# First passes behind the fourth and fifth norm over tiles without the root, and gate sums as two scans

## The chip, the cores and the metric

The kernel runs on one core of one Trainium2 chip. Its time is device time in microseconds. TensorE (PE) multiplies matrices and writes PSUM, VectorE (DVE) and ScalarE (ACT) do the elementwise work, GpSimd (POOL) adds a few squares, and SyncE (SP) issues the loads of the weights. Each engine works through its own list in a fixed order, and semaphores join the lists.

## The reference

Two blocks run one after the other on 256 tokens of width 1024, all in float32. The part that matters begins at the end of the first block: its last feed-forward (`ffn2`), its final norm, then the first (even) layer of the second block and the start of its second (odd) layer.

```python
x = x + 0.5 * ml[8] * swiglu(modulate(rms_norm(x, norm3_g), ml[6], ml[7]), ffn2_w_in, ffn2_w_out)
x = rms_norm(x, final_g)
...
def even_layer(x, ...):                       # second block, layer 0
    h = rmsnorm(x, pre_g)                     # the fourth norm
    u = h @ w_in
    qa, ka, va, oa, za, ia, fa, qb, kb, vb, zb = split_cols(u, EVEN_SPLITS)
    qk = silu(causal_dwconv(concatenate([qa, ka]), conv_w))
    ig = ia + b_i
    lf = log_sigmoid(fa + b_f)
    ha = mlstm(qa, ka, va, ig, lf)            # 4 heads: running sum of lf, running maximum
    ...
    return x + rmsnorm(y @ w_out, post_g)     # the post norm
def odd_layer(x, ...):                        # second block, layer 1
    h = rmsnorm(x, pre_g)                     # the fifth norm
    p, z = split(h @ w_in)                    # p is pooled over windows of 2, 4, 8, 16 tokens
    ...
```

A norm multiplies each token by one number, 1/root(mean of squares). A product with weights is linear, so that number may multiply the product instead of the input.

## The kernel before

**Products.** Channels lie on partitions and tokens along the free dimension. Each float32 operand is split into a high part (type fp32r) and the rest, and a product is three matmuls: high by high, low by high, high by low. A load brings 512 rows by 256 columns of a weight, a chunk, into one of six slots of `W`. The step `split` makes it usable: ACT copies it to `WH` (line 1298), DVE subtracts that to give `WL` (line 1645). `WH` and `WL` hold four chunks, so ACT's copy of a chunk waits until PE has finished the chunk four places back. With 8 rows of 128 inputs, a product of 256 columns takes two chunks of 24 matmuls each. PSUM banks 0 to 3 hold the product tiles in turn (`plan.tiles`), banks 4 to 6 the small work, bank 7 (`NB`) the sums of squares.

**The list.** The class `Plan` writes one list of steps, and every engine walks it and takes out its own part. `gemm` emits the chunks of one product, keeps the splits three to four chunks ahead (`LOOK`), and after each chunk calls `tick`, which takes one step of the generators in `self.back` (at most three in turn). `drain` runs them all to their end, with no chunk between.

**The fourth norm.** The last `fx2` tiles (feed-forward 2) are added into `X` by DVE (line 1528). ACT squares them twice (`square`, line 1129), PE sums the squares over the partitions with a matrix of ones (`ones`, line 842). The step `norm` follows: PE fills the time with seven matmuls that nobody reads (`warm`, line 899) and waits for the roots; ACT, DVE and ACT take the two roots (the final norm and the fourth norm follow each other, so there are two); DVE takes the reciprocal (line 1761), then writes eight times x by scale by reciprocal into `TS` (line 1492), ACT copies each to `XH` (line 1143), DVE subtracts to give `XL` (line 1500). Only then come the gates' 24 matmuls with 8 columns (`gr`, lines 1011 to 1013), and the products `eq`, `ek`, `ev`, `eo`, `ez` of head 0, 48 matmuls each, then those of heads 1 to 3.

**The gates.** The generator `gates` moves the gate rows through the steps g0, g1 (line 1017 on PE, then Abs, Exp, Ln on ACT at lines 1397 to 1401), three steps g2 (running sum by eight shifted additions, line 1632), three g3 (running maximum, likewise) and g4 (two small transposes, line 1022). Beside it runs `final_x` (nine steps that scale `X` by the final norm, line 1778). The generator `mlstm` of a head starts when g4 is done: m0 (lines 1029 to 1038), two ticks later m1 (1045 to 1053), five later m2 (1058). `drain` is called at the end of each head's products from head 1 on.

**The fifth norm.** Behind the output product `p0` the step `post` normalises the product: DVE multiplies by the reciprocal (line 1789) and adds to `X` (line 1795), ACT squares, PE sums; `norm` again makes the root and eight normalised tiles. Then come the products `op` (to be pooled, DVE lines 1588 to 1601, then `PH` and `PL`), `oz` (to `OZ`), 48 matmuls each, and after six of them the mixing product `om` from `PH` and `PL`.

## Time and profile before

| | us |
|---|---|
| median of 3 runs (lowest, highest) | 1418.59 (1418.24, 1421.0) |
| the profiled execution, its own time | 1421.97 |
| its span, first to last instruction | 1420.2 |
| PE busy | 1351.3 |
| DVE busy | 904.4 |
| ACT busy | 647.6 |

The profile is of one execution. Its time stands 3.4 us above the median; 1.8 us of it lie outside the span. A matmul row's duration overlaps that of its neighbours, so the distance of starts counts, not the duration. "PEclk" is the granted clock of TensorE as a share of 2.4 GHz: 1.00 is 2.4 GHz, 0.50 is 1.2 GHz. A row names what ended the idle time before it in brackets.

### The profile page before, as it was taken

What the parts mean: (1) busy time and instruction counts of PE and PEld (TensorE: products, weight loads), DVE (VectorE), ACT (ScalarE), POOL (GpSimd) and SP (SyncE); (2) the same over time, 40 slices, a digit from 0 to 9 for tenths busy, and PEclk for the clock granted to TensorE, in tenths of its full rate; (3) what the DMA queues carried; (4) which work ended last, traced back from release to release, by engine and by line L of the source; (5) the groups of instructions that cost most, each with busy time, mean ns of one, the idle gap of its engine ahead of it and who ended that gap; (6) DMA issues with size and microseconds to landing.
All of it is one profiled execution on the core that took longest, in us unless ns stands there. A gap on an engine that the chain in (4) does not pass through costs nothing.

```text
span 1420.2 us, 23299 instructions
## 1 busy us (share of the span) xinstructions
PE 1351.3 (95%) x9344; PEld 1224.1 (86%) x9344; DVE 904.4 (64%) x1448; ACT 647.6 (46%) x1017; POOL 25.2 (2%) x29
## 2 busy tenths in 40 slices
PE   6999999999997999999999999899899999999996
PEld 3688888888886799999989999788899999999996
DVE  3546456653476477766776655688776665487864
ACT  3522221222244335455554444565665765465553
POOL 0000000000100000000000000100000000000000
PEclk7999999999999999999999999999999999999998
DMA  7743434634344244366747765465345554536561
GB/s 260 263 147 119 149 133 148 193 104 155 119 157 133 75 142 153 124 206 225 266 162 240 240 190 177 119 178 163 106 146 150 149 155 127 164 119 192 181 196 42
DMA packets 201403, 229.67 MB, mean 162 GB/s; under 512 B 7120, under 2 KB 191696, under 8 KB 201296
## 3 DMA queue, kind: packets, MB, share of 16 engines
q1 hardware_dynamic: 201008, 227.90, 50.7%
q8 instruction: 74, 1.21, 0.4%
q10 hardware_dynamic: 288, 0.29, 0.1%
q14 instruction: 33, 0.27, 0.1%
HBM read 227.11 MB, written 1.05 MB: 161 GB/s over the span
## 4 chain that ended last, share of the span: by engine, by line
PE 54%; DVE 7%; ACT 3%; DMA 3%; issue 2%; SPq 0%; POOL 0%; ACTq 0%; DVEq 0%; POOLq 0%
PE P L880 15%; PE P L881 14%; PE P L882 14%; DMA W<-in_ffn_w_in 2%; ACT WH L1298 2%; PE P L886 1%; PE P L888 1%; PE P L887 1%; DVE WL L1645 1%; PE P L1001 1%; PE P L989 1%; PE P L842 1%; DVE TS L1492 1%; PE P L994 0%; PE P L972 0%
## 5 line engine op out<-in xcount | busy, mean ns | idle before, releaser
L1645 DVE TENSOR_TENSOR WL<-W,WH 128x1024 fp32r<-128x1024 f32 x358 | 432.1, 1220 | 302.7 <-ACT WH L1298 301.8
L880 PE MATMUL P<-XH,WH 128*128 128x256 f32 (+1 forms) x1808 | 560.1, 310 | 9.2 <-DVE XL L1502 4.2
L881 PE MATMUL P<-XL,WH 128*128 128x256 f32 (+1 forms) x1808 | 546.9, 303 | 0.0
L882 PE MATMUL P<-XH,WL 128*128 128x256 f32 (+1 forms) x1808 | 546.6, 302 | 0.0
L1298 ACT ACTIVATE WH<-W 128x1024 fp32r<-128x1024 f32 x358 | 368.9, 1043 | 249.1 <-PE P L882 128.4
L880 PEld LDWEIGHTS P<-XH,WH 128*128 128x128 f32 x1808 | 342.6, 189 | 36.8 <-issue 14.4
L881 PEld LDWEIGHTS P<-XL,WH 128*128 128x128 f32 x1808 | 341.6, 189 | 19.8 <-issue 2.9
L882 PEld LDWEIGHTS P<-XH,WL 128*128 128x128 f32 x1808 | 341.4, 189 | 17.1
L880 PE MATMUL P<-GH,WH 128*128 128x256 f32 (+1 forms) x372 | 123.0, 331 | 0.0
L882 PE MATMUL P<-GH,WL 128*128 128x256 f32 (+1 forms) x372 | 122.3, 329 | 0.0
L881 PE MATMUL P<-GL,WH 128*128 128x256 f32 (+1 forms) x372 | 122.3, 329 | 0.0
L880 PEld LDWEIGHTS P<-GH,WH 128*128 128x128 f32 x372 | 70.0, 188 | 7.4 <-DVE WL L1645 0.3
L881 PEld LDWEIGHTS P<-GL,WH 128*128 128x128 f32 x372 | 70.1, 188 | 7.1 <-issue 0.2
L882 PEld LDWEIGHTS P<-GH,WL 128*128 128x128 f32 x372 | 70.0, 188 | 6.9
L1168 ACT ACTIVATE GH<-TS 128x512 fp32r<-128x512 f32 (+1 forms) x44 | 22.7, 526 | 107.5 <-DVE TS L1518 107.5
L1709 DVE CUSTOM_DVE_ANT_0 W<-W,AC,V 128x1024 f32<-128x1024 f32 x56 | 71.6, 1279 | 0.0
L1518 DVE TENSOR_TENSOR TS<-TS,P 128x512 f32<-128x512 f32 (+1 forms) x44 | 23.9, 552 | 66.0 <-PE P L882 66.0
L1162 ACT ACTIVATE TS<-P 128x512 f32<-128x512 f32 (+1 forms) x44 | 21.0, 488 | 74.0 <-PE P L882 74.0
L1103 POOL TENSOR_TENSOR SQ<-SQ 128x256 f32<-128x256 f32 (+1 forms) x25 | 25.0, 1000 | 1373.2 <-ACT SQ L1129 1372.1
L886 PE MATMUL P<-WH,XH 128*128 128x256 f32 x160 | 46.3, 290 | 0.0
L887 PE MATMUL P<-WL,XH 128*128 128x256 f32 x160 | 45.6, 285 | 0.0
L888 PE MATMUL P<-WH,XL 128*128 128x256 f32 x160 | 45.5, 285 | 0.0
(290 smaller groups left out, 1816.6 us busy)
## 6 DMA issues: line engine op xcount, KB each, us to landing
W<-in_ffn_w_in SPq DMA_DIRECT2D x88, 512.0 KB, 5.5
W<-in_w_in_ab SPq DMA_DIRECT2D x72, 512.0 KB, 3.8
W<-in_w_modt SPq DMA_DIRECT2D x56, 512.0 KB, 4.0
W<-in_w_in SPq DMA_DIRECT2D x52, 512.0 KB, 4.5
W<-in_ffn_w_out SPq DMA_DIRECT2D x40, 512.0 KB, 4.8
W<-in_w_in_c SPq DMA_DIRECT2D x32, 512.0 KB, 4.0
W<-in_w_mod SPq DMA_DIRECT2D x16, 512.0 KB, 4.7
W<-in_w_out_ab SPq DMA_DIRECT2D x16, 512.0 KB, 3.6
```

What stands on the lines that cost most here:

```text
L880: pe.matmul(o, h[:, k, c], xh[:, kk, a:b], start=kk == 0, stop=False)
L881: pe.matmul(o, h[:, k, c], xl[:, kk, a:b], start=False, stop=False)
L882: mm = pe.matmul(o, l[:, k, c], xh[:, kk, a:b], start=False, stop=kk == gm.nk - 1)
L886: pe.matmul(o, xh[:, kk, c], h[:, k, :], start=kk == 0, stop=False)
L887: pe.matmul(o, xh[:, kk, c], l[:, k, :], start=False, stop=False)
L888: mm = pe.matmul(o, xl[:, kk, c], h[:, k, :], start=False, stop=kk == gm.nk - 1)
L1103: pool.tensor_tensor(SQ[:, 0, 0:n], SQ[:, 0, 0:n], SQ[:, 1 + (k - 1) % 2, 0:n], ALU.add) \
L1168: act.activation(GH[m][:, f % 12, :], TS[:, f % NS, 0:n], ACT.Copy).then_inc(S[f"hh{m}"], 1)
L1298: act.activation(h, a, ACT.Copy).then_inc(S["wh"], 1)
L1518: dve.tensor_tensor(TS[:, f % NS, 0:n], TS[:, f % NS, 0:n], ps, ALU.mult).then_inc(S[f"hm{m}"], 1)
L1645: dve.tensor_tensor(l, a, h.bitcast(F32), ALU.subtract).then_inc(S["wl"], 1)
L1709: td = dve.tensor_tensor_reduce(a if v == s.c - 1 else JK[:, :, :], a, (AC0, AC1)[v][:, :, :], 1.0, vec("bmod", 8 * g + k), ALU.mult, ALU. ...
```

## The change

- While `fx2` ends, ACT and DVE also make `XH` and `XL` (their columns 0 to 255, free at that time) from x by scale, without the root: the function `raw`. `eq` and `ek` of head 0 and the gates' rows run over these (type `raw` of the Gemm). So do `op` and `oz` of group 0 behind the fifth norm, where the step `pk` joins the additions of `post` with `raw`.
- Each of these eight tiles, and the gates' rows, is multiplied by the reciprocal when DVE takes it out of PSUM (`rooted`, line 1629 of the new file, and step g0), and ACT then works from SBUF.
- The normalised tiles are still made, four at a time (step `nm`), in between, for the products that follow. `warm` behind the fourth and the fifth norm is gone; behind the post norm ten of them stay in one piece.
- The gates' running sum and maximum are one scan instruction each; g2 and g3 are one step. The memory that is cleared for them shrinks. Of the two gate chunks only 8 columns are split.
- `final_x` starts after the fourth head's generator is added.

```diff
+    def even_start(self, eq, ek, ce, cg, ck):
+
+        self.half(eq, 0, ce[0], -1)
+        self.half(eq, 4, ce[1], 0)
+        self.step("o4")
+        self.half(eq, 4, ce[1], 1, 0)
+        self.step("r4")
+        self.nb_free = ("tw", 2)
+        self.split_chunk(ck[0])
+        b, f = self.bank(("gfree", 1))
+        for c, j in enumerate(cg):
+            self.marks += 1
+            self.chunk_end[j] = self.marks
+            self.step("gr", chunk=j, k0=4 * c, nk=4, bank=b, free=f)
+        self.ended("gr")
+        self.back.append(self.gates(b))
+        self.step("rx", gemm=eq)
+        self.split_chunk(ck[1])
+        self.tick()
+        self.step("nm", a=4, b=0)
+        self.half(ek, 0, ck[0], -1)
+        self.tick()
+        n = self.chunks[ck[1]][0]
+        self.split_to(n + 1)
+        self.step("nm", a=4, b=4)
+        self.half(ek, 4, ck[1], -1, 0)
+        self.tick()
+        self.split_to(n + 2)
+        self.step("ev", gemm=eq)
+        self.step("cvt", gemm=eq)
+        self.step("rx", gemm=ek)
+        self.tick()
+        self.split_to(n + 3)
+        self.step("cvr", gemm=eq)
+        self.step("ev", gemm=ek)
+        self.step("cvt", gemm=ek)
+        self.tick()
+        self.step("cvr", gemm=ek)
...
+        self.post(0)
+        self.step("pk", a=0)
+        self.half(op[0], 0, cp[0], -1)
+        self.step("pk", a=4)
+        self.half(op[1], 0, cp[1], -1)
+        self.split_chunk(cp[3])
+        self.split_chunk(cz[0])
+        self.step("o6", a=0)
+        self.half(op[0], 4, cp[2], -1, 0)
+        self.step("o6", a=4)
+        self.split_chunk(cz[1])
+        self.step("r5", b=self.root("n", 5))
+        self.half(op[1], 4, cp[3], -1, 0)
+        self.step("rx", gemm=op[0])
+        self.split_chunk(cz[2])
+        self.half(oz[0], 0, cz[0], -1)
+        self.step("ev", gemm=op[0])
+        self.step("rx", gemm=op[1])
+        self.step("nm", a=5, b=0)
+        self.split_chunk(cz[3])
+        self.half(oz[0], 4, cz[1], -1, 0)
+        self.step("opp", gemm=op[0])
+        self.step("rx", gemm=oz[0])
+        self.step("ev", gemm=oz[0])
+        self.step("nm", a=5, b=4)
+        self.half(oz[1], 0, cz[2], -1)
+        n = self.chunks[cz[3]][0]
+        self.split_to(n + 1)
+        self.step("ev", gemm=op[1])
+        self.half(oz[1], 4, cz[3], -1, 0)
+        self.step("opp", gemm=op[1])
+        self.split_to(n + 2)
+        self.step("rx", gemm=oz[1])
+        self.step("ev", gemm=oz[1])
+        self.split_to(n + 3)
...
-            self.gemm("ev", h, WAB, 0, 8, 2048 + 256 * h, LAT, turned=False)
+            if h:
+                self.gemm("eq", h, WAB, 0, 8, 256 * h, LAT)
+                self.gemm("ek", h, WAB, 0, 8, 1024 + 256 * h, LAT)
+            self.gemm("ev", h, WAB, 0, 8, 2048 + 256 * h, LAT, turned=False, first=h == 0)
             self.gemm("eo", h, WAB, 0, 8, 3072 + 256 * h, LAT)
             self.gemm("ez", h, WAB, 0, 8, 4096 + 256 * h, LAT)
             if h:
                 self.call(self.drain)
             self.call(lambda h=h: self.back.append(self.mlstm(h)))
+        self.call(lambda: self.back.append(self.final_x()))
...
-        for i in range(3):
-            self.step("g3", a=i)
-            yield
+        self.step("g2")
...
+            def raw(k, scale):
+
+                act.activation(XH[:, k, 0:T], X[:, k, 256:512], ACT.Copy, scale=scale).then_inc(S["xh"], 1)
...
+                                act.wait_ge(S["am"], 4)
+                                raw(k, AM[:, 2, 1, k:k + 1])
...
+            def raw(q, k, scale):
+
+                dve.wait_ge(S["xh"], q + 1)
+                dve.scalar_tensor_tensor(XL[:, k, 0:T], X[:, k, 256:512], scale, XH[:, k, 0:T].bitcast(F32), ALU.mult,
+                                         ALU.subtract).then_inc(S["xr"], 1)
...
+            def rooted(gm):
+
+                kind, i = gm.kind, gm.i
+                dve.wait_ge(S["dv"], inverse)
+                for j, t in enumerate(gm.tiles):
+                    k = 2 * i + j
+                    dve.wait_ge(S["g"], plan.tile_end[t])
+                    if kind[0] == "e":
+                        c = 2 * (kind == "ek") + j
+                        dve.wait_ge(S["gz"], 1)
+                        if c >= 3:
+                            dve.wait_ge(S["cvs"], c - 2)
+                        o = CV[:, c % 3, 3:T + 3]
+                    elif kind == "op":
+                        if k >= 2:
+                            dve.wait_ge(S["opc"], k - 1)
+                        o = PV[:, 3 * (k % 2), 16:16 + T]
+                    else:
+                        o = OZ[:, k, :]
+                    dve.tensor_tensor(o, P[:, t % 4, 0:T], RS[:, 0, 256:512], ALU.mult).then_inc(S["rx"], 1)
...
+                elif s.kind == "r4":
+                    r2 = RS[:, 0, 256:512]
+                    dve.wait_ge(S["on"], stat["s4"][2] + 3)
+                    dve.tensor_copy(r2, NB[:, T:2 * T]).then_inc(S["dv"], 1)
+                    own += 1
+                    dve.wait_ge(S["dv"], own)
+                    dve.scalar_tensor_tensor(r2, NB[:, 0:T], EPS, r2, ALU.mult, ALU.add).then_inc(S["two"], 1)
+                    dve.wait_ge(S["tw"], 1)
+                    dve.reciprocal(r2, r2).then_inc(S["dv"], 1)
+                    own += 1
+                    inverse = own
+                elif s.kind == "r5":
+                    r = RS[:, 0, 256:512]
+                    dve.wait_ge(S["sr"], s.b)
+                    dve.reciprocal(r, r).then_inc(S["dv"], 1)
+                    own += 1
+                    inverse = own
+                elif s.kind == "nm":
+                    dve.wait_ge(S["dv"], inverse)
+                    dve.wait_ge(S["am"], 4)
+                    dve.wait_ge(S["g"], end["hx", 2] if s.a == 4 else end["even"])
+                    tiles(s.a, s.b, s.b + 4, lambda k: vec("pre1", k) if s.a == 5 else AM[:, 2, 1, k:k + 1],
+                          lambda k: None, RS[:, 0, 256:512])
...
+                elif s.kind == "pk":
+                    for k in range(s.a, s.a + 4):
+                        add(0, k)
+                        if k > s.a:
+                            raw(7 + k, k - 1, vec("pre1", k - 1))
+                    raw(8 + k, k, vec("pre1", k))
...
+                    ig, b, t2, top, neg = (G[:, i, 128:384] for i in range(5))
+                    dve.wait_ge(S["gfree"], 1)
+                    dve.tensor_scalar(top, b, 0.0, None, ALU.min).then_inc(S["dv"], 1)
+                    own += 1
+                    dve.wait_ge(S["dv"], own)
+                    dve.wait_ge(S["gab"], 3)
+                    dve.tensor_tensor_scan(b, top, t2, 0.0, ALU.add, ALU.subtract).then_inc(S["dv"], 1)
+                    own += 1
+                    dve.wait_ge(S["dv"], own)
+                    dve.wait_ge(S["gr0"], 2)
+                    dve.tensor_tensor(t2, ig, b, ALU.subtract).then_inc(S["gq"], 1)
+                    dve.wait_ge(S["gq"], 1)
+                    dve.tensor_tensor_scan(top, t2, t2, 0.0, ALU.max, ALU.max).then_inc(S["dv"], 1)
+                    own += 1
+                    dve.wait_ge(S["dv"], own)
+                    dve.tensor_scalar(neg, top, -1.0, None, ALU.mult).then_inc(S["dv"], 1)
+                    own += 1
+                    dve.wait_ge(S["dv"], own)
+                    dve.tensor_tensor(G[:, 5, 128:384], neg, b, ALU.subtract).then_inc(S["gq"], 1)
```

**ACT, the gates of the even layer.** `WH` is a chunk's split, `Ev`, `Ek`, `TS`, `XH` are tiles as above, `G` the gates' rows. Before:

```order
L1298 ACTIVATE WH<-W 128x1024 [waits s_g,s_w5]
L1409 ACTIVATE Ek<-TS 128x256 [waits s_cvs] x2
L1397 ACTIVATE G<-G 4x256 [waits s_gfree]
L1399 ACTIVATE G<-G 4x256 [waits s_gab]
L1401 ACT_TABLE_LOAD
L1401 ACTIVATE G<-G 4x256 [waits s_gab]
L1298 ACTIVATE WH<-W 128x1024 [waits s_g,s_w0]
L1230 ACTIVATE Ev<-P 128x256 [waits s_g] x2
```

Now (`s_nt` counts the tiles that DVE has scaled in `nm`, `s_gfree` is DVE's step g1):

```order
L1378 ACTIVATE WH<-W 128x1024 [waits s_g,s_w1]
L1217 ACTIVATE XH<-TS 128x256 [waits s_nt,s_g]
L1217 ACTIVATE XH<-TS 128x256 [waits s_nt] x3
L1485 ACTIVATE G<-G 4x256 [waits s_gfree]
L1487 ACT_TABLE_LOAD
L1487 ACTIVATE G<-G 4x256 [waits s_gab]
L1489 ACT_TABLE_LOAD
L1489 ACTIVATE G<-G 4x256 [waits s_gab]
L1378 ACTIVATE WH<-W 128x1024 [waits s_g,s_w2]
L1217 ACTIVATE XH<-TS 128x256 [waits s_nt,s_g]
L1217 ACTIVATE XH<-TS 128x256 [waits s_nt] x3
```

The gates' three functions now stand between the two halves of the normalised tiles and ahead of the split of `ev`'s first chunk (`s_w2`), with two table loads instead of one.

**PE, the same place.** Before, the small product of step g1 is followed by `ev` (the rows with `WH` on the left); the transposes of g4 stand 385 rows later:

```order
L880 MATMUL P<-XH,WH 128x256
L881 MATMUL P<-XL,WH 128x256
L882 MATMUL P<-XH,WL 128x256
L1017 MATMUL P<-TS,C 4x256 [waits s_gr0]
L886 MATMUL P<-WH,XH 128x256 [waits s_cve,s_wl]
L887 MATMUL P<-WL,XH 128x256
L888 MATMUL P<-WH,XL 128x256
```

Now the second half of `ek` follows g1, and g4 stands ahead of `ev`:

```order
L959 MATMUL P<-XH,WH 128x256
L960 MATMUL P<-XL,WH 128x256
L961 MATMUL P<-XH,WL 128x256
L1091 MATMUL P<-TS,C 4x256 [waits s_gr0]
L959 MATMUL P<-XH,WH 128x256 [waits s_wl]
L960 MATMUL P<-XL,WH 128x256
L961 MATMUL P<-XH,WL 128x256
...
L1096 MATMUL P<-C,G 128x4 [waits s_gq,s_at]
L965 MATMUL P<-WH,XH 128x256 [waits s_nl,s_rx,s_wl]
L966 MATMUL P<-WL,XH 128x256
L967 MATMUL P<-WH,XL 128x256
```

`ev` now stands behind the transposes, which wait (`s_gq`) for the subtraction that follows the first scan on DVE.

**DVE, start of the odd layer.** Rows from the splits to the second product. `X`, `V`, `RS` are input, scale and reciprocal, `PV` the pooled tile, `PL` and `OZ` as above. Before:

```order
L1500 TENSOR_TENSOR XL<-TS,XH 128x256 [waits s_nh] x2
L1645 TENSOR_TENSOR WL<-W,WH 128x1024 [waits s_wh]
L1651 MEMSET PV 128x1632 [waits s_g]
L1645 TENSOR_TENSOR WL<-W,WH 128x1024 [waits s_wh,s_pvz]
L1588 TENSOR_TENSOR PV<-PV 128x256 [waits s_ope]
L1595 TENSOR_TENSOR TS<-PV,C 128x1 [waits s_dv]
L1598 SCALAR_TENSOR_TENSOR TS<-PV 128x255
L1601 TENSOR_TENSOR TS<-TS,PV 128x1 [waits s_dv]
L1588 TENSOR_TENSOR PV<-PV 128x256 [waits s_ope]
L1595 TENSOR_TENSOR TS<-PV,C 128x1 [waits s_dv]
L1598 SCALAR_TENSOR_TENSOR TS<-PV 128x255
L1601 TENSOR_TENSOR TS<-TS,PV 128x1 [waits s_dv]
```

Now, from the second tile pair of `rooted` on (rows with `RS` and `P`):

```order
L1629 TENSOR_TENSOR PV<-P,RS 128x256 [waits s_opc,s_g,s_dv]
L1629 TENSOR_TENSOR PV<-P,RS 128x256 [waits s_opc,s_g]
L1580 SCALAR_TENSOR_TENSOR TS<-X,V,RS 128x256 [waits s_g,s_am,s_dv]
L1580 SCALAR_TENSOR_TENSOR TS<-X,V,RS 128x256
L1589 TENSOR_TENSOR XL<-TS,XH 128x256 [waits s_nh]
L1580 SCALAR_TENSOR_TENSOR TS<-X,V,RS 128x256
L1589 TENSOR_TENSOR XL<-TS,XH 128x256 [waits s_nh]
L1580 SCALAR_TENSOR_TENSOR TS<-X,V,RS 128x256
L1589 TENSOR_TENSOR XL<-TS,XH 128x256 [waits s_nh] x2
L1780 TENSOR_TENSOR WL<-W,WH 128x1024 [waits s_wh]
L2106 TENSOR_TENSOR PL<-TS,PH 128x256 [waits s_ph] x2
L1629 TENSOR_TENSOR OZ<-P,RS 128x256 [waits s_g,s_dv]
```

Before, all eight normalised tiles come first and splits and pooling follow; now four normalised tiles stand between two `rooted` pairs, and the split behind them (`s_wh`) comes after.

## Rows read from the trace of the kernel before

**Rows 1.** Page, section 1: busy time, share of the span, instructions of each engine.
```profile
PE 1351.3 (95%) x9344; PEld 1224.1 (86%) x9344; DVE 904.4 (64%) x1448; ACT 647.6 (46%) x1017; POOL 25.2 (2%) x29
```

**Rows 2.** Waits of PE, whole run: idle us, count, mean of one.
```profile
PE P L1017 <- DVE G L1837: 2.8, 1, 2.8
```

**Rows 3.** Windows: us, then busy (count) of PE, PEld, DVE, ACT, POOL; PEclk; DMA share; GB/s.
```profile
907.20:916.00 8.80, 5.30 (x19) 3.25 (x19) 5.01 (x11) 3.25 (x8) 0.00 (x0) 1.00 0.28 82
935.50:942.20 6.70, 6.70 (x29) 5.85 (x30) 6.56 (x13) 2.69 (x7) 0.00 (x0) 0.51 0.56 157
944.70:966.40 21.70, 21.70 (x194) 21.70 (x193) 19.16 (x33) 15.06 (x24) 0.00 (x0) 1.00 0.61 172
983.00:997.50 14.50, 9.61 (x35) 7.50 (x34) 8.72 (x19) 4.84 (x10) 0.00 (x0) 0.74 0.31 90
1027.20:1031.00 3.80, 3.76 (x15) 3.43 (x16) 2.13 (x2) 1.96 (x3) 0.00 (x0) 0.55 0.78 245
1235.80:1251.10 15.30, 13.65 (x63) 11.03 (x61) 11.16 (x22) 5.78 (x14) 0.00 (x0) 1.00 0.11 35
1251.10:1285.20 34.10, 34.10 (x289) 34.08 (x290) 28.69 (x59) 21.58 (x36) 0.00 (x0) 1.00 0.54 165
```

**Rows 4.** Timeline of PE: start, duration, instruction, [idle before it, what ended that].
```profile
908.66 1.98 PE L842 MATMUL P<-SQ,C 128*128 128x512 f32 x4 [1.43 <-ACT SQ L1129]
936.43 0.58 PE L886 MATMUL P<-WH,XH 128*128 128x256 f32 x1
1001.52 0.69 PE L1029 MATMUL P<-G,C 4*128 4x256 f32 x2
1038.10 0.69 PE L1029 MATMUL P<-G,C 4*128 4x256 f32 x2
1073.34 0.69 PE L1029 MATMUL P<-G,C 4*128 4x256 f32 x2
```

**Rows 5.** Timeline of DVE around the fourth norm (last row: first norm of the block).
```profile
911.18 0.42 DVE L1746 COPY RS<-P 128x256 f32<-128x256 f32 x1 [3.04 <-ACT RS L1344]
912.64 1.75 DVE L1761 RECIPROCAL RS<-RS 128x256 f32<-128x256 f32 x1 [0.57 <-ACT RS L1347]
915.80 0.48 DVE L1492 SCALAR_TENSOR_TENSOR TS<-X,AM,RS 128x256 f32<-128x256 f32 x1
916.53 0.48 DVE L1492 SCALAR_TENSOR_TENSOR TS<-X,AM,RS 128x256 f32<-128x256 f32 x1
925.73 3.41 DVE L1645 TENSOR_TENSOR WL<-W,WH 128x1024 fp32r<-128x1024 f32 x3
930.74 2.85 DVE L1570 SCALAR_TENSOR_TENSOR TS<-CV,V,TS 128x256 f32<-128x256 f32 x6
952.85 1.30 DVE L1632 TENSOR_TENSOR G<-G 4x256 f32<-4x256 f32 x3
781.07 0.74 DVE L1518 TENSOR_TENSOR TS<-TS,P 128x256 f32<-128x256 f32 x2
```

**Rows 6.** Timeline of ACT: a split of the first part of a chunk, then the gates.
```profile
933.95 1.04 ACT L1298 ACTIVATE WH<-W 128x1024 fp32r<-128x1024 f32 x1
942.06 0.42 ACT L1397 ACTIVATE G<-G 4x256 f32<-4x256 f32 x1 [1.10 <-DVE G L1841]
942.94 1.28 ACT L1401 ACT_TABLE_LOAD   x1
944.24 0.42 ACT L1401 ACTIVATE G<-G 4x256 f32<-4x256 f32 x1
```

**Rows 7.** Timeline of DVE at the start of the odd layer.
```profile
1239.44 0.43 DVE L1789 TENSOR_TENSOR X<-X,RS 128x256 f32<-128x256 f32 x1
1240.25 0.42 DVE L1789 TENSOR_TENSOR X<-X,RS 128x256 f32<-128x256 f32 x1
1260.53 0.42 DVE L1588 TENSOR_TENSOR PV<-PV 128x256 f32<-128x256 f32 x1
1261.47 0.42 DVE L1588 TENSOR_TENSOR PV<-PV 128x256 f32<-128x256 f32 x1
```

More of the change, by code:

```diff
@@ L99 @@
     first: bool
+    raw: bool = False
     tiles: list = field(default_factory=list)
@@ L261, in mod_part, with half @@
         self.prog.append(run)
-    def half(self, gm, k0, j, h):
-        if k0 == 0 and h == 0:
+    def half(self, gm, k0, j, h, a=1):
+        if k0 == 0 and h < 1:
             base = len(self.tile_end)
@@ L277, in half, with freed, split_chunk @@
             self.chunk_end[j] = self.marks
-        self.step("ck", gemm=gm, k0=k0, nk=4, chunk=j, a=int(last), half=h)
+        self.step("ck", gemm=gm, k0=k0, nk=4, chunk=j, a=int(last and a), half=h)
+    def freed(self, gm):
+        if not gm.raw:
+            return self.up(self.EVICT[gm.kind])
+        if gm.kind != "op":
+            self.up(self.EVICT[gm.kind])
+        return self.up("rx")
+    def split_chunk(self, j):
+        self.split_to(self.chunks[j][0])
+    def even_start(self, eq, ek, ce, cg, ck):
[35 more added lines that the diff above has]
+        self.step("cvr", gemm=ek)
@@ L517, in ended, with norm @@
         self.end[name[0] if len(name) == 1 else name] = self.marks
-    def norm(self, n, scale=0, row=0):
-        if scale:
-            self.step("scales", a=scale, b=row)
-        if n == 4:
-            self.nb_free = ("two", 1)
-        else:
-            self.root("n", n)
+    def norm(self, n, scale, row):
+        self.step("scales", a=scale, b=row)
+        self.root("n", n)
         self.step("norm", a=n, b=len(self.tile_end) % 4)
@@ L533, in post @@
         self.step("post", a=i, b=len(self.tile_end) % 4)
-    def gate_rows(self, parts):
-        b, f = self.bank(("gfree", 1))
-        for c, j in enumerate(parts):
-            n = self.chunks[j][0]
-            self.split_to(n + LOOK)
-            self.marks += 1
-            self.chunk_end[j] = self.marks
-            self.step("gr", chunk=j, k0=4 * c, nk=4, bank=b, free=f)
-            self.split_to(n + LOOK + 1)
-        self.ended("gr")
-        self.back.append(self.gates(b))
     def ffn(self, n, win, wout, cols):
@@ L637, in gates @@
         yield
-        for i in range(3):
-            self.step("g2", a=i)
-            yield
-        for i in range(3):
-            self.step("g3", a=i)
-            yield
+        self.step("g2")
         yield
@@ L841, in ones @@
                     pe.wait_ge(S[nb[0]], nb[1])
-                pe.matmul(NB[:, 0:n], con("one"), SQ[:, slot, 0:n], start=i == 0, stop=i == parts_ - 1) \
+                pe.matmul(NB[:, 0:n], con("one"), SQ[:, slot, c:c + n], start=i == 0, stop=i == parts_ - 1) \
                     .then_inc(S["on"], 1)
@@ L864, in chunk @@
                         pe.wait_ge(S[name], v)
-                    if gm.first and j == 0:
+                    if gm.first and j == 0 and kind != "oz":
                         if kind in ("fa1", "fb1"):
@@ L963, in _ @@
                         pe.wait_ge(S["sr"], plan.roots["post", 0])
-                        warm(4, s.b)
-                        for i in range(6):
-                            ones("s6", i)
-                            warm(1, s.b)
+                        warm(7, s.b)
                 elif s.kind == "qa":
@@ L1621, in evict @@
                                                  ALU.subtract).then_inc(S["o2l"], 1)
+                    elif kind == "fx2" and g == 12:
+                        dve.wait_ge(S["am"], 4)
+                        raw(i + j, i + j, AM[:, 2, 1, i + j:i + j + 1])
                     elif kind == "om":
```

296 lines of the change are left out of this document (139 added, 157 removed), and 2 rows, old and new, of the table names.

## Prediction

> **What bounds the kernel now.** I read the page's busy shares first. TensorE is busy 1351.3 of 1420.2 us, DVE 904.4 and ACT 647.6 [rows 1], so the end is set by PE's list, and a change can give time only where PE idles or runs at half clock. Then the windows around both seams, for PE's busy time and its granted clock [rows 3]. With nothing late PE does a matmul of 256 columns every 0.113 us (192 in 21.7 us, clock 1.00). The fourth norm: fx2 ends at 907.2, the sums of squares at 910.6 [rows 4], the reciprocal at 914.39 and the eight tiles go at 0.73 us each [rows 5]; the gates' rows then crawl with them. The 8.8 us to 916.0 hold no product at all, only two sums of squares (2 us) and warm-ups. Later PE idles 2.8 us before the gates' small product [rows 2], after which the clock is 0.51 for 6.7 us [rows 3]. From 983.0 to 997.5 PE is busy 9.6 us at clock 0.74: mlstm of head 0, run whole in a drain because the gates' generator ended too late. The fifth norm: 1235.8 to 1251.1 hold `warm` and sums of squares, no product, then 288 matmuls of `op`, `oz` and `op` of group 1 run without a gap at clock 1.00 to 1285.2 [rows 3]. These seams are what the change can win: at most about 7 + 10 us at the first, 10 at the second.
>
> **The first seam, part by part** (clock of the profiled run of before). Raw tiles: `raw` adds eight ACT and eight DVE steps of about 0.4 us beside fx2's long chunks; PE is the late one there, so nothing. The first part of `eq`, 36 matmuls at 0.113, runs from 907.2 to 911.3. The two sums of squares, 1.98 [rows 4], end at 913.3. Copy to end of reciprocal is 914.39 - 911.18 = 3.2 [rows 5]: 916.6. DVE does one queued `WL` (1.14, from 3.41 for three [rows 5]), 917.8, and the first `rooted` pair, 0.74 [rows 5]. In ACT's list the second chunk of `ek`'s split stands behind that, so `WH` (1.04 [rows 6]) and `WL` come at 921.4, g0 at 922.3, and PE pauses about 2 us in `ek`. Next in DVE's list, ahead of g1's outcome, are four tiles of `nm` (4 x 0.73 = 2.9, 3.5 with hops): 925.8, then g1's addition. ACT's Abs, Exp and Ln follow: 944.66 - 942.06 = 2.6 [rows 6], with one more table load of 1.28 because ACT was just at copies of another table: 3.9, 930.1. Only behind these does ACT's list have the split for `ev` (front, order of ACT): `WH` 931.2, `WL` 932.4, then the second four tiles, 935.9. Then minimum, scan and subtraction, three steps at 0.43 (1.30 for three [rows 5]): 937.2. PE has had the last half of `ek` by 925.6 and waits from there, about 12 us, since `ev` stands behind the transposes of g4 in its list. `ev` starts near 937.7; before, it started at 936.43 [rows 4].
>
> So the 5 us that the raw tiles bring in front, and the warm-ups that go, are spent again on a queue: the gates stand in the way of `ev`. What follows is `ev`, 48 matmuls, at half clock after such a pause; before, they took 936.43 to 944.7, 8.3 us [rows 3, 4]: 946.0. Then `eo` waits for its split behind the second scan, `rooted` of `ek` and two convolutions of 2.85 [rows 5]: the first chunk of `eo` is split at 946.0 and the second at 952.2 (scan 0.4, `WL` 1.14, conv 2.85, rooted 0.74, ACT 0.8, `WH` 1.04, `WL` 1.14; then `cvr` 0.74, conv 2.85, tanh 0.45, `WH` 1.04, `WL` 1.14). From there to m0, which is taken behind the first chunk of head 1, are 96 matmuls (24 of `eo`, 48 of `ez`, 24 of `eq`), 10.9 us: 963.1; half clock behind the pauses costs half of 3.8 to half of 6.7 us [rows 3], I take 2.5: 965.6. That is where m0 of head 0 can start: the gates' generator is done, so mlstm of head 0 runs between head 1's chunks like its successors, and not in the drain. From m0 of one head to m0 of the next is 1073.34 - 1038.10 = 35.24, or 1038.10 - 1001.52 = 36.58 [rows 4]. m0 of head 1 then stands at 1000.8; before, at 1001.52. **Term 1: -0.7 us**, -3.2 (less penalty, half a us less in each hop) to +1.5 (the longer period, 36.58, and a little).
>
> The scans replace 16 shifted additions and maxima of 0.43 by two instructions. The trace of before has no scan. Bounds: as an addition of the same shape, 0.43 [rows 5], or as the slowest row of that length, a reciprocal, 1.75. I take 0.43, whose shape it has. One of them is on the path to `ev`: +0 to +1.3.
>
> The Trainium skill ("DVE: opcode table, instruction layouts, handler registers and perf-mode slots", § 6. Datapath and trigger behaviour) states that a scan runs at half the throughput of ordinary two-input work; worked out as an estimate by that page it would add 0.3 us each. No row here shows it.
>
> **`final_x` moved to the end of head 3.** Its nine steps (a reciprocal of 1.75, eight scalings of 0.4) lie beside 48-matmul products now as then, but most of them may fall in the drain ahead of the ssm groups. DVE is at 19 of 21.7 us busy there in the window from 944.7 [rows 3], so it is not free: **+0.5**, 0 to 1.5.
>
> **The second seam.** The reciprocal of `post` ends at 1239.4. A `pk` step is two additions, 0.81 (1240.25 - 1239.44 [rows 7]), and a raw subtraction, 0.4: 1.2 per tile. `op` starts at 1241.6 (before: 1251.1), and its first 24 matmuls go with the tiles, at most one input row per 1.2 us where three matmuls need 0.34 per row and product: 1245.3. The second tile of four rows gives 1248.05, four sums of squares 1249.8, second chunk 1252.6, four more sums 1254.4, last chunk of the second product 1257.2. Thus 96 matmuls stand before 1257.2, where before 52 of them were done by then (6.1 us at 0.118); PE leads by about 5 us. Then the root: 0.47 and 1.75, 1256.9; first `rooted` pair 1257.6, `WL` 1258.7, two pool tiles at 0.94 (1261.47 - 1260.53 [rows 7]) 1260.6, second `rooted` pair 1261.3, four `nm` tiles 1264.8. Only then is the split for the last chunk of `oz` done: ACT's copy waits for PE's `WH` buffer and ends with the tiles, `WL` 1266.6 (DVE's order in front: `s_wh` behind four `nm` tiles); `PL` and `rooted` 1268.0; four `nm` tiles 1271.5, the next split 1273.3. PE has been through 192 matmuls at 1269.5 and waits 3.85 us. Two pool tiles, `PL`, the split of `op`'s second chunk 1277.9, `rooted`, SiLU, the split of the second product 1281.2; PE waits for each. 48 more matmuls, 5.5: 1286.8 for the 288th, before 1285.2: +1.6. Half clock behind those waits adds 0 to 1. **Term 2: +2 us.** In order, the loads change place too: `eq`'s two chunks now come ahead of the gates' two, and the odd layer's first six go `op`, `op`, `oz`. DMA share is 0.11 to 0.28 in those windows [rows 3], so no load is late: 0. DVE here has 16 more operations of 0.4 (8 raw, 8 `rooted`: 6.4 us) less a memset of 1.4: the engine, not PE, now sets this stage, since before it was busy 28.7 of 34.1 us [rows 3]. Bounds: +0.6 (no clock loss, hops 1 us less) to +5, where the clock also falls in the first pass, with gaps of 0.5 to 0.9 us per row.
>
> **Sum.** -0.7 + 0.5 + 2 = +1.8 us on the profiled execution's own 1421.97 us, so 1423.8 for a run like that. The median of three stands 3.4 us lower, 1418.59: 1420.4.
>
> **Rivals.** (A) The forecast: stalls move, one off against the other, -1 to +5: 1417.6 to 1423.6.
>
> (B) Faster. DVE and ACT lists interleave better than I add up: the pause before `ev` is 4 us, not 12 (2.9 for each four tiles hidden behind `ek`, loads one instead of two), its clock penalty is gone, and the waits of 3.85 + 3 us in the second seam shrink. That returns 8 + 2 us and 4 + 3, 17 in all: 1420.4 - 17 = 1403.4; with only part of it, up to 1413. For it: 5 us were won by eq in front, and 14.5 us of drain with 9.6 of PE's work at clock 0.74 [rows 3] leave the path. Against it: each order is fixed, and the steps named stand ahead in it.
>
> (C) Slower. The clock. Gaps between matmuls of `op`'s first pass, 0.5 to 0.9 us per row with nothing to keep PE warm (`warm` is gone), bring 0.5 for the 15 us from 1241.6. 96 matmuls then take twice 0.113 each, 10.9 us more, most of it inside the gaps: +4; and the clock penalty at the first seam is the 3.35 of its upper end, not 2.5: +0.85. 1420.4 + 4.85 = 1425.3. It decides if the windows of 1241 to 1257 show a granted clock under 0.8. For it: 0.51 to 0.55 after pauses of about 2.5 us; against it: 1.00 from 907.2 to 916 with pauses of 0.7 to 1.4 us [rows 3, 4].
>
> (D) The table loads. In the row, Exp ends just ahead of the load and Ln starts at its end, 944.24: 1.28 us [rows 6], with no drain. If a load cost more where the gates now have two, `ev` would start later by that: at twice the row's price, +1.3 each, +2.6: 1423.0. The Trainium skill ("ScalarE: Activation LUTs", § What ACT_TABLE_LOAD costs) puts a switch at the load and about as much again for the drain; by that page's figures the two switches would take 2.8 us longer, an estimate, which this row speaks against.
>
> (E) The change doesn't do what it says: scans gain nothing, since the gates wait for ACT's tables and the reciprocal, not for additions. That is part of A already: only 1 scan is on the path.
>
> **Numbers.** A 0.42, B 0.28, C 0.23, D 0.07. 0.2% (2.8 us) is about what a measurement of this kernel can tell from no change, so within 1415.8 to 1421.4 is the same. A gives 0.33 same, 0.08 slower and 0.01 faster; B 0.28 faster; C 0.20 slower and 0.03 same; D 0.04 slower and 0.03 same: faster 0.29, same 0.39, slower 0.32. Range: from inside B, 1409 (two thirds of what it returns), to the upper end of C with the bounds of scan and clock, 1427; 0.15 of the chance lies below and 0.04 above. A's own range is 1417 to 1424.
>
> **What would show it.** In the trace of the changed kernel: an idle row of PE before the transposes of g4 and `ev`, released by DVE's `G`, of about 12 us; a window behind it at half clock; m0 of head 0 between head 1's chunks, at 965 or so, and no busy window of 14 us like 983 to 997.5. In the odd start: `op` from 1241.6; pauses of PE before `oz`'s last chunk and `op` of group 1, released by `WL`; PEclk 1.00 in the first pass (A) or near 0.5 (C). An `ev` at 930 or before and `op` of group 1 without pause would make B right. What would break the forecast most is a step of my two lists that does not wait for its neighbour as I think, 1 to 3 us each.

## The result and the profile after

The changed kernel takes 1423.43 us (median of 16 runs, 1421.7 to 1428.53), the kernel before 1421.0 (median of 16 runs, 1418.24 to 1426.66). The ratio is 1.0023, 95% interval 1.0012 to 1.0034: slower by 3.3 us (1.7 to 4.8). (The medians are 2.4 us apart, the means 3.4.) Five of the changed kernel's 16 runs lie apart from the others, at 1427.3 to 1428.5, and the other eleven between 1421.7 and 1424.6. The profiled execution of the changed kernel took 1423.3 us against 1421.97 of before, so the two traces explain 1.3 us of it.

Page of the changed kernel, busy time (beside [rows 1]):

```profile
PE 1344.4 (95%) x9310; PEld 1221.3 (86%) x9310; DVE 906.6 (64%) x1460; ACT 648.4 (46%) x1025; POOL 25.0 (2%) x29
```

PE has 7 us less work (34 matmuls fewer, all of them warm-ups) and idles more. What it waits for, whole run (us in total, times, longest; beside [rows 2]):

```profile
PE P L959 <- DVE WL L1780: 12.6, 13, 3.5
PE P L1096 <- DVE G L1997: 9.6, 1, 9.6
...
PE P L959 <- DVE TS L1747: 2.6, 2, 1.7
...
PE P L1091 <- DVE G L1980: 1.4, 1, 1.4
```

The wait of 2.8 us for the gates' small product became 1.4 us there and 9.6 us before the transposes of g4. The windows of the changed kernel (columns as in [rows 3]):

```profile
925.80:935.68 9.88, 0.29 (x4) 0.12 (x2) 5.72 (x13) 7.21 (x11) 0.00 (x0) 0.63 0.18 53
935.95:942.20 6.25, 6.25 (x30) 6.25 (x30) 5.52 (x12) 1.59 (x5) 0.00 (x0) 0.51 0.30 84
983.00:997.50 14.50, 12.69 (x102) 12.24 (x101) 9.02 (x13) 9.85 (x16) 0.00 (x0) 1.00 0.55 160
1237.87:1290.24 52.37, 45.74 (x352) 43.89 (x353) 45.52 (x103) 28.30 (x54) 0.00 (x0) 0.97 0.39 122
```

The drain at 983 is gone: 102 matmuls at full clock where before there were 35 instructions at 0.74. The price is the pause of 9.6 us before `ev`, the half clock behind it, and an odd start in which DVE is busy 45.5 of 52.4 us. PE's timeline at the marks of the prediction (beside [rows 4]):

```profile
935.68 0.23 PE L1096 MATMUL P<-C,G 4*128 4x4 f32 x1 [9.59 <-DVE G L1997]
935.95 0.58 PE L965 MATMUL P<-WH,XH 128*128 128x256 f32 x1
950.76 0.38 PE L959 MATMUL P<-XH,WH 128*128 128x256 f32 x1 [3.11 <-DVE WL L1780]
961.85 0.48 PE L1103 MATMUL P<-G,C 4*128 4x256 f32 x1
997.09 0.48 PE L1103 MATMUL P<-G,C 4*128 4x256 f32 x1
...
1237.87 0.36 PE L959 MATMUL P<-XH,WH 128*128 128x256 f32 x1 [0.24 <-DVE XL L1607]
...
1269.26 0.38 PE L959 MATMUL P<-XH,WH 128*128 128x256 f32 x1 [3.48 <-DVE WL L1780]
...
1282.71 0.28 PE L959 MATMUL P<-PH,WH 128*128 128x256 f32 x1
1290.24 0.36 PE L959 MATMUL P<-XH,WH 128*128 128x256 f32 x1 [1.70 <-DVE TS L1747]
```

Rows 961.85 and 997.09 are m0 of heads 0 and 1; before, m0 of head 1 stood at 1001.52 [rows 4]. `op` starts at 1237.87 (before: 1251.08), but the mixing product of group 0 at 1282.71 (before: 1285.17, 288 matmuls behind `op` in both) and the product behind it at 1290.24 (before: 1290.85). The reciprocal of `post` starts at 1233.86 (before: 1237.66), so the odd start lost 1.3 us up to `om` and 1.9 more before the product behind it. DVE and ACT at the gates (beside [rows 5, 6]):

```profile
924.21 0.47 DVE L1984 TENSOR_SCALAR G<-P,V 4x256 f32<-4x256 f32 x1
929.56 1.22 DVE L1780 TENSOR_TENSOR WL<-W,WH 128x1024 fp32r<-128x1024 f32 x1 [4.88 <-ACT WH L1378]
...
934.10 0.27 DVE L1989 TENSOR_SCALAR G<-G 4x256 f32<-4x256 f32 x1
934.41 0.68 DVE L1993 TENSOR_TENSOR_SCAN G<-G 4x256 f32<-4x256 f32 x1
935.12 0.41 DVE L1997 TENSOR_TENSOR G<-G 4x256 f32<-4x256 f32 x1
```

```profile
924.71 0.42 ACT L1485 ACTIVATE G<-G 4x256 f32<-4x256 f32 x1 [0.87 <-DVE G L1984]
925.14 1.28 ACT L1487 ACT_TABLE_LOAD   x1
926.44 0.41 ACT L1487 ACTIVATE G<-G 4x256 f32<-4x256 f32 x1
926.87 1.28 ACT L1489 ACT_TABLE_LOAD   x1
928.16 0.41 ACT L1489 ACTIVATE G<-G 4x256 f32<-4x256 f32 x1
928.49 1.04 ACT L1378 ACTIVATE WH<-W 128x1024 fp32r<-128x1024 f32 x1
```

This is the queue of the prediction, step by step: g1 on DVE at 924.21; ACT is in the gates from 924.71 to 928.57, two loads of 1.28 us among it; only then `WH` of `ev`; DVE idles 4.88 us for it, makes `WL` and four tiles; the scan starts at 934.41 though its input was there at 928.57.

### The profile page after: what moved, and what is told of

It is laid out like the page before. It is cut to its first block, busy times and chain, and to the rows that moved or that the text cites. A ratio compares the mean times of both kernels' runs of the same rounds, so it can differ in the third digit from the quotient of the medians.

```text
span 1421.5 us, 23263 instructions
## 1 busy us (share of the span) xinstructions
PE 1344.4 (95%) x9310; PEld 1221.3 (86%) x9310; DVE 906.6 (64%) x1460; ACT 648.4 (46%) x1025; POOL 25.0 (2%) x29
## 4 chain that ended last, share of the span: by engine, by line
PE 54%; DVE 7%; ACT 4%; issue 3%; DMA 2%; SPq 0%; ACTq 0%; DVEq 0%
PE P L959 15%; PE P L961 14%; PE P L960 14%; ACT WH L1378 2%; DMA W<-in_ffn_w_in 2%; DVE WL L1780 1%; PE P L965 1%; PE P L967 1%; PE P L966 1%; PE P L1075 1%; PE P L1063 1%; PE P L921 1%; DVE TS L1580 1%; DVE PV L1730 1%; PE P L1068 0%
```

## The experiments

Ratios are against the kernel before, run beside it on the same chip. Executions of one list differ by some us ahead of the place that is looked at, so the traces are compared by distances: A is from the last matmul row of `fx2` to m0 of head 1, B from the last row of `p0` to the first `om` and C from there to the second `om` group. (C holds 48 + 192 matmuls and their waits.) All in us, from PE's timelines:

| kernel | ratio, 95% interval | fx2 to ev | A: fx2 to m0 of head 1 | B | C |
|---|---|---|---|---|---|
| before | 1 | 29.5 | 94.6 | 49.5 | 27.5 |
| changed | 1.0023 (1.0012 to 1.0034) | 29.9 | 91.1 | 50.9 | 30.2 |
| e1_scans | 0.9941 (0.9926 to 0.9956) | 29.1 | 86.0 | 48.4 | 27.5 |
| e11_one_tick | 0.9986 (0.9974 to 0.9998) | 29.3 | 91.6 | 48.4 | 27.5 |
| e7_g1_later | 0.9923 (0.9905 to 0.9941) | 25.6 | 82.9 | 48.4 | 27.5 |
| e2_even | 1.0010 (0.9996 to 1.0023) | 29.9 | 92.7 | 49.5 | 27.5 |
| e3_gates_behind | 1.0024 (1.0012 to 1.0036) | 20.1 | 92.7 | 50.8 | 29.4 |
| e4_even_behind | 0.9989 (0.9976 to 1.0002) | 20.1 | 91.5 | 48.4 | 27.5 |
| e9_gates_between | 0.9987 (0.9976 to 0.9997) | 20.1 | 87.1 | 50.9 | 30.2 |
| e10_even_between | 0.9944 (0.9927 to 0.9962) | 20.1 | 87.1 | 49.5 | 27.5 |
| e5_warm | 1.0022 (1.0009 to 1.0035) | 29.8 | 91.1 | 50.8 | 30.2 |
| e8_oz_no_root | 1.0022 (1.0010 to 1.0034) | 29.9 | 95.5 | 49.6 | 28.1 |

Each row is one execution, and a list doesn't take the same time in each. The changed kernel, e2_even and e8_oz_no_root have one and the same list over all of A, and A is 91.1, 92.7 and 95.5; the seven kernels with the odd start of before have B at 48.4 or at 49.5. (Where these differences lie is said at the end.) So a difference of A under 4 us, or of B about 1, says little by itself; the distance from `fx2` to `ev` is 29.9 in all three.

**The scans alone.** Edit to the kernel before, and with it the DVE code of the changed kernel for g2:

```diff
-        for i in range(3):
-            self.step("g2", a=i)
-            yield
-        for i in range(3):
-            self.step("g3", a=i)
-            yield
+        self.step("g2")
+        yield
```

> The kernel before, with the gates' running sum and maximum as two scans in one step (g2 and g3 together), nothing else of the change. Theory T (the gain of the change is the mlstm of head 0 that leaves the drain, and the scans alone bring it): g4 is done while head 0 runs, the 14.4 us of PE between 983.31 and 997.68 go, its matmuls come back inside head 1's chunks with about 7 us, so m0 of head 1 stands about 7.5 us earlier than at 1001.5 and the ratio to before is 0.995. Rival R (DVE, busy 19 of 21.7 us there, gives the gain back): waits of PE for WL in head 1 eat it, ratio 0.998 to 1.000. In both, a scan of 4 x 256 takes 0.68 us.

Measured 0.9941: 8.4 us faster than before, what the theory expected and a little more. DVE's and PE's timeline of this kernel:

```profile
949.70 0.68 DVE L1846 TENSOR_TENSOR_SCAN G<-G 4x256 f32<-4x256 f32 x1
950.42 0.41 DVE L1850 TENSOR_TENSOR G<-G 4x256 f32<-4x256 f32 x1
950.87 0.68 DVE L1852 TENSOR_TENSOR_SCAN G<-G 4x256 f32<-4x256 f32 x1
```

```profile
964.41 0.46 PE L1025 MATMUL P<-G,C 4*128 4x256 f32 x1
994.06 0.48 PE L1025 MATMUL P<-G,C 4*128 4x256 f32 x1
```

m0 of head 0 comes at 964.41 and that of head 1 at 994.06 instead of 1001.52, as the theory had it (7.5 us). The scans take 0.68 us each, and PE has none of the theory's rival's waits for `WL` up to there. So the change holds one part that gains 8 us, and the rest of it, the raw tiles above all, loses more than that.

**Fewer steps or shorter steps.** The gates' list may gain since g2 and g3 take one tick in place of six, or since the scans are short. Edit to the kernel before: the `yield` behind each of the six steps g2 and g3 goes, one stays behind the last; all 16 shifted operations stay.

> The kernel before with its 16 shifted additions and maxima kept, but the six steps g2 and g3 taken by one tick instead of six, so that g4 and m0 of head 0 stand in TensorE's list where e1_scans has them. Theory A (the gain of the scans is that mlstm of head 0 leaves the drain; how long DVE takes for them is covered): ratio to before 0.995, within 0.0015 of e1_scans (0.9941), though DVE works 5.5 us more at that place. Rival B (the scan's shorter time matters): a wait of PE of 2 to 5 us behind the 16 operations, ratio 0.997 to 0.998.

Measured 0.9986. Theory A falls in its "within 0.0015 of e1_scans"; B is right, and somewhat too small. g4 and m0 stand in the same row of PE's list in both kernels (m0 of head 0 has 312 product matmuls behind `fx2` in front of it in both, and 480 in the kernel before), but DVE is busy with the block from 947.6 to 956.7, 9.1 us against 2.9 in e1_scans, and the split behind it is late (PE's timeline):

```profile
957.92 0.39 PE L879 MATMUL P<-XH,WH 128*128 128x256 f32 x1 [3.84 <-DVE WL L1644]
968.08 0.46 PE L1028 MATMUL P<-G,C 4*128 4x256 f32 x1
```

Of the 8.5 us that A gives in e1_scans (94.6 to 86.0), 3.0 are there with one tick alone and 5.5 come with the short instructions. Both are needed: one tick takes mlstm of head 0 out of the drain, and the short block keeps that from being paid for at the next split.

**The odd start as before.** e2_even is the changed kernel with `post`, `norm` and the first `op` of before put back.

> The changed kernel with the start of the odd layer as before (post, warm-ups, eight normalised tiles, then op), and the start of the even layer and the scans as changed. T: the odd start costs what the two traces show between the reciprocal of post and the end, 5.1 us (1.3 up to om, 1.9 before om's second chunk, 1.9 of pace), so this one is about 4 us faster than before: ratio 0.997. Rival R: the 5.1 us are in part the pace of single executions and not of the list; ratio 0.999 to 1.000.

Measured 1.0010: 1.8 us under the changed kernel, nearer to the rival. The same exchange was made at two other orders of the even start (below): 1.0024 to 0.9989 and 0.9987 to 0.9944, which are 5.0 and 6.1 us. The three together give 4.3 us for the raw odd start, each with an uncertainty of 2 to 3. In the traces, B + C are 80.2 to 81.1 us in the four kernels with it and its full work, and 75.9 to 77.0 in the seven without. Windows from the start of `op` to `om`, and from there to the next `om` group, of the changed kernel and then of e2_even:

```profile
1237.87:1282.71 44.84, 39.91 (x305) 38.23 (x305) 38.13 (x85) 25.01 (x48) 0.00 (x0) 0.96 0.36 110
1282.71:1312.93 30.22, 28.52 (x243) 28.35 (x241) 25.27 (x49) 16.75 (x28) 0.00 (x0) 1.00 0.62 196
```

```profile
1248.33:1282.42 34.09, 34.09 (x289) 34.07 (x289) 27.24 (x58) 21.69 (x36) 0.00 (x0) 1.00 0.56 169
1282.42:1309.89 27.47, 27.47 (x243) 27.47 (x241) 22.50 (x45) 15.74 (x26) 0.00 (x0) 1.00 0.59 182
```

PE has no gap in e2_even and 4.9 + 1.7 in the changed kernel. The 10 us by which `op` starts earlier are all given back, and 4 on top.

**Is it DVE's load?** e8_oz_no_root is the changed kernel with ACT taking `oz` of group 0 from PSUM, without the multiplication by the reciprocal:

```diff
-                elif s.kind == "rx":
+                elif s.kind == "rx" and s.gemm.kind != "oz":
                     rooted(s.gemm)
...
-                        act.activation(OZ[:, k, :], OZ[:, k, :] if gm.raw else ps, ACT.Silu).then_inc(S["oze"], 1)
+                        act.activation(OZ[:, k, :], ps, ACT.Silu).then_inc(S["oze"], 1)
```

> The changed kernel in which oz of group 0 is not multiplied by the reciprocal: ACT takes it straight from PSUM (this part of the computation is left out), so DVE has four operations of 0.37 us less in the odd start. T (DVE's queue sets the odd start): the wait before the second chunk pair of om in group 0 (1.7 us for DVE's L1747) and the waits for WL shrink by the 1.5 us, from p0's end to the first om 49.5 to 50 us instead of 50.8, ratio to before 1.001. Rival: the order (splits behind normalised tiles), not DVE's load, sets it: no more than 0.3 us, ratio 1.002.

The ratio, 1.0022, is on the rival's side and tells nothing finer than about 2 us. In the trace the waits in the stretch (for `WL` and for DVE's L1747) shrank from 4.5 and 1.7 us to 3.1 and 0.4, which is more than the 1.5 us of DVE work left out. B is 49.6, where the theory had 49.5 to 50, and B + C fell from 81.1 to 77.7; 0.9 of that is the pace of the matmuls in C (see the end), not a wait. So the trace bears the theory out, the whole run doesn't show it. That the odd start hangs on how much DVE has in its list is likely, not shown.

**The gates out of ev's way.** e3_gates_behind takes four of the five ticks out of `even_start`:

```diff
         self.half(ek, 0, ck[0], -1)
-        self.tick()
         n = self.chunks[ck[1]][0]
...
         self.half(ek, 4, ck[1], -1, 0)
-        self.tick()
         self.split_to(n + 2)
...
         self.step("rx", gemm=ek)
-        self.tick()
...
         self.step("cvt", gemm=ek)
-        self.tick()
         self.step("cvr", gemm=ek)
```

> The changed kernel with g1, g2 and g4 of the gates taken by the ticks of ev's and eo's chunks instead of those in even_start (only g0 stays there). T (the 9.6 us wait before ev is the gates' place in ACT's and PE's list and nothing else): ev starts at 926 to 927 instead of 935.95, about 5 us of that are left at m0 of head 0 since eo's splits still wait for two convolutions, ratio to before 0.999. Rival R (DVE's convolutions set the time of eo anyway): m0 of head 0 within 1 us of 961.85, ratio 1.0015 to 1.0025.

> Both of the last two: odd start as before, gates behind ev's first chunk. T: the effects add, 4 + 5 us below before, ratio 0.994. Rival R: as for the two alone, 0.998 to 1.000.

`ev` starts 9.8 us earlier, as the theory had it (20.1 us behind `fx2`), and nothing is left of that: m0 of head 0 stands at 964.11, A is 92.7, the ratio 1.0024 (the rival's). PE's timeline of e3_gates_behind:

```profile
926.64 0.38 PE L961 MATMUL P<-WH,XH 128*128 128x256 f32 x1 [2.83 <-DVE WL L1776]
938.15 0.58 PE L955 MATMUL P<-XH,WH 128*128 128x256 f32 x1 [3.27 <-DVE WL L1776]
952.66 0.23 PE L1092 MATMUL P<-C,G 4*128 4x4 f32 x1 [5.32 <-DVE G L1993]
964.11 0.48 PE L1099 MATMUL P<-G,C 4*128 4x256 f32 x1
```

`eo` starts at 938.15 (changed kernel: 944.56), but now DVE's scans stand behind both pairs of convolutions and g4 waits 5.3 us, which neither the theory nor its rival had. e4_even_behind is the same with the odd start as before: A 91.5, the ratio 0.9989, where the theory had 0.994 and the rival 0.998 to 1.000. Beside e2_even (1.0010) it is 3 us faster, whereas e3_gates_behind isn't faster than the changed kernel; each of these two comparisons is good to about 2.5 us, so up to that much may still have come of the move. The wait moved from ahead of `ev` to ahead of g4. To see whether any order helps, e9 puts the steps apart: `tick` for g1 behind the splits of both chunks of `ev`, `tick` for g2 behind `rooted` of `ek`, g4 behind `ev`'s second chunk.

> The changed kernel with the gates' steps placed apart: ACT's Abs, Exp and Ln (g1) behind the splits of both chunks of ev, DVE's scans (g2) behind the first convolutions, g4 on TensorE behind ev's second chunk. In e3_gates_behind g4 was waited for at 952.66 (5.3 us) and the clock fell; here g2 stands 5 us earlier. Theory T (every loss of the raw start is such a place in a list): ev starts 20 us behind the end of fx2 and g4 is not waited for, m0 of head 0 48 to 50 us behind the end of fx2 (55.8 in the changed kernel), ratio to before 0.998. Rival R (the chain from the roots over the convolutions to eo's splits is as long in any order): m0 of head 0 not under 54 us, ratio 1.001 to 1.002.

> The same, with the start of the odd layer as before (as e2_even). T: 3 to 5 us below e9_gates_between, since the odd start's raw tiles cost that much, ratio to before 0.995, and so no better than the kernel before with the scans alone (0.994). Rival: the raw start of the odd layer costs under 2 us; the two stand within 0.0015 of each other.

```profile
928.39 0.38 PE L963 MATMUL P<-WH,XH 128*128 128x256 f32 x1 [2.34 <-DVE WL L1778]
933.54 0.39 PE L963 MATMUL P<-WH,XH 128*128 128x256 f32 x1 [0.89 <-DVE WL L1778]
939.15 0.25 PE L1094 MATMUL P<-C,G 4*128 4x4 f32 x2 [2.51 <-DVE G L1995]
942.86 0.58 PE L957 MATMUL P<-XH,WH 128*128 128x256 f32 x1 [3.46 <-DVE WL L1778]
```

Those are the waits of e9 from `ev` on. m0 of head 0 is 51.9 us behind `fx2` (55.8 in the changed kernel): between the theory's 48 to 50 and the rival's 54, and g4 is still waited for (2.51). The ratio came down from 1.0023 to 0.9987, so 5 us of the raw start's loss are the places in the lists. And e10 at 0.9944 is level with e1_scans at 0.9941: even in the best order that was tried, the raw start of the even layer brings nothing over the plain one (A 87.1 against 86.0).

**Is the half clock a price?** e5_warm puts 20 warm-up matmuls in the pause before `ev`.

```diff
         self.half(ek, 4, ck[1], -1, 0)
+        self.step("hot", b=eq.tiles[0] % 4)
         self.tick()
...
+                elif s.kind == "hot":
+                    pe.wait_ge(S["rx"], 2)
+                    warm(20, s.b)
```

> The changed kernel with 20 warm-up matmuls on TensorE in the 9.6 us in which it waits for the gates before ev (nothing reads them). They keep the clock up: the rows of ev take 0.113 to 0.118 us each instead of 0.21 for the first 6 us. Theory T (behind ev the splits of eo, held by DVE's convolutions, set the time, not PE): ev ends 3 us earlier, the wait before eo grows by as much, ratio to before unchanged at 1.002. Rival C (the half clock is a price of its own): 3 us come off, ratio 1.000.

Measured 1.0022, and A is 91.1 to the tenth. The window of this kernel over `ev` has a clock of 1.00, against 0.51 in the changed one:

```profile
936.60:944.50 7.90, 5.44 (x47) 5.23 (x45) 6.13 (x12) 2.61 (x5) 0.00 (x0) 1.00 0.24 68
```

PE's timeline behind it has the time saved as a wait of 2.77 us at `eo`'s first chunk, where the changed kernel has none:

```profile
944.80 0.38 PE L960 MATMUL P<-XH,WH 128*128 128x256 f32 x1 [2.77 <-DVE WL L1784]
951.01 0.38 PE L960 MATMUL P<-XH,WH 128*128 128x256 f32 x1 [1.58 <-DVE WL L1784]
```

The second chunk starts 6.2 us behind the first in both kernels (950.76 - 944.56 and 951.01 - 944.80), set by its split; PE waits 3.11 us for it in the changed kernel at a clock of 1.00, and 1.58 here at 0.73. So behind the pause the splits of `eo` are late, not PE, and half clock in `ev` costs nothing.

**A version that beats both.** e7_g1_later is e1_scans with g1 taken three ticks later (behind `ev`'s first chunk) and `final_x` behind head 3 (with it, m2 no longer waits for `final_x`):

```diff
         self.step("g0", bank=bank)
-        yield
+        for _ in range(4):
+            yield
```

> The kernel before with the scans (as e1_scans), with final_x started behind head 3 as in the change, and with step g1 of the gates behind the first chunk of ev instead of ahead of ev. T: the wait of 2.8 us before the gates' small product and the half clock behind it (2 us) go as well: m0 of head 1 some 4 us earlier than in e1_scans against the end of fx2 (86.0 us there), ratio to before 0.991. Rival R (the splits behind the convolutions were the next to be late): waits for WL take its place, 0.5 to 1 us gained over e1_scans, ratio 0.9935.

Measured 0.9923, 10.9 us under before and between the theory's 0.991 and the rival's 0.9935. The wait of 2.8 us before the gates' small product is gone; behind the gates' rows PE has two short new ones up to m0 of head 1, 0.8 us at g4 and 0.3 us for ACT's `Ev`, and none for `WL`. The clock is 1.00 from `ev` to m0 of head 0. A at 82.9 is 3.2 us shorter than in e1_scans, all of it (29.1 to 25.6) ahead of `ev`. The two intervals of the ratio overlap, so of the gain over e1_scans only the trace speaks, and the two edits were not taken apart: `final_x` out of the way also gives its ticks to the gates.

## Why the prediction came out as it did

The forecast was 1.8 us slower than before with a main case of stalls that move; measured were 3.3 (1.7 to 4.8), within the range and on the side forecast. By its steps:

- **The queue before `ev`** stood as worked out: ACT in the gates 3.9 us (measured 924.71 to 928.57, 3.86), `WH`, `WL`, four tiles, three DVE steps, a pause of about 12 us (9.6), `ev` at 937.7 (935.95). The steps on ACT and DVE ran 1.5 to 1.8 us earlier, 0.9 of it because `fx2` ended earlier in this execution, and PE was through `ek` half a us later than I had it (926.1, not 925.6).
- **The scan** was taken at 0.43 us by the row of a shifted addition; it takes 0.68, inside the bounds. The Trainium skill ("DVE: opcode table, instruction layouts, handler registers and perf-mode slots", § 6. Datapath and trigger behaviour) has it at half throughput; the row agrees: 0.68 beside 0.41 for an operation of the same shape in the same list.
- **The two table loads** took 1.28 us each, with Exp's end at 926.85 and the load's start at 926.87. Rival D falls; the Trainium skill ("ScalarE: Activation LUTs", § What ACT_TABLE_LOAD costs) has a drain as long again, and this trace shows none.
- **Term 1** was -0.7 us at m0 of head 1 and came out at -4.4 (997.09 against 1001.52), outside its bounds of -3.2 to +1.5; without the earlier end of `fx2` it is -3.5 (A: 94.6 to 91.1), still just outside. 1.4 of the difference came with the earlier `ev` and was still there at `eo`'s second chunk (952.2 forecast, 950.76 measured); the other 2.3 are most of the 2.5 us that I had put down for half clock behind the pauses of `eo`. In this execution the clock was back at 1.00 after 942.2 and stayed there. In others with the same list it fell again, and the piece was 1.6 and 3.1 us (below), so it was mis-sized for the profiled execution rather than for the kernel.
- **Term 2** was +2 and came out at +3.2 by 1290 and about +5 at the end. Up to `om` the sum held (+1.3, forecast +1.6), but not piece by piece: behind the wait of 3.85 us (3.48) I had two more of 2.5 together, and one of 0.35 came; in their place PE took 13.45 us for the last 96 matmuls, at a granted clock of 0.87 on the mean, about 2 us more than at 0.113 each and the one wait. The step that failed is the end of it: I let the sum stop at the 288th matmul, and the wait of 1.7 us for DVE's L1747, pushed by the same queue, came next. Behind it come another 1.9 us of pace (below); whether the change has a part in that is open.
- **`final_x`** was +0.5. From m0 of head 3 to `p0` are 107.3 us before and 107.5 after: 0.2.
- **Rival E, that scans gain nothing, was taken into the main case wrongly.** I wrote that the scans gain nothing because one of them is on the path to `ev`. Alone they gain 8.4 us. I had seen where they gain (mlstm out of the drain) and counted it to the whole change, so the sum came out near right while its parts did not, which was in part luck: it hid a gain of 8 us beside losses of about 6 in the raw even start (A: 86.0 to 91.1 to 92.7) and 4 in the raw odd start.
- **Rivals B and C.** The pause before `ev` was 9.6 us and not 4, and `op` of group 1 was waited for 3.48 us (B). The window from 1241 to 1257, which was to decide on C, has a granted clock of 1.00; from the start of `op` to `om` it is 0.96 on the mean, and not 0.5.

What stays open: the traces give +1.3 us and the comparison of 32 runs +3.3. The five runs of the changed kernel at 1427.3 to 1428.5 make 1.6 us of its mean, and no trace is of one of them; the kernel before has one such run in 16 (1426.66).

## What to carry to other kernels

Price each part of a bundle as if it were the only one. Moving the root behind the product starts PE earlier but leaves every normalised tile to be made as well; where PE's next products hang on splits, gates and tiles in DVE's and ACT's lists, the early start is a loan from these queues. Before shortening a side chain, look at which drain or tick it ends in: here sixteen short operations on DVE in six ticks decided over 8 us, since behind them hung a whole attention step in a stretch with no product beside it. Taking the ticks away without shortening the work gave 3.0 of the 8.5 us of A (2.0 of the 8.4 us of the whole run); the rest needed the short block. And carry the hand sum on until the next engine to be late is one that was late before as well.
